# Reordering the output products, the rotation and the low parts around a layer's attention

## The chip, the cores and the metric

One core of a Trainium2 chip runs the whole program. The metric is the device time of one execution in microseconds; the number compared is the median of several executions.

## The reference, cut to what matters

The reference is a two-layer block followed by a second block (dilated attention, an RWKV mixer and a mixture of experts). The change touches only the two layers. One of them computes, for 256 tokens of width 1024 in float32:

```python
for l in range(2):
    h = rmsnorm(x, g_mix[l])
    cq, ckv, kr, aq, ak, av, qi, ki, wi, rq, rk, rv, rg = split(h @ w_in[l])
    q  = rmsnorm(cq, g_q[l]) @ w_uq[l]           # 8 heads of 64 + 32 rotated channels
    kv = rmsnorm(ckv, g_kv[l]) @ w_ukv[l]
    o_a = mla_attention(q, kv, rope(kr))         # 8 heads, 512 columns, causal softmax
    o_b = dsa_attention(aq, ak, av, top-64 keys by qi, ki, wi)   # 4 heads, 256 columns ("sparse")
    o_c = silu(rg) * head_groupnorm(retention(rq, rk, rv))       # 4 heads, 256 columns
    x = x + concat(o_a, o_b, o_c) @ w_out[l]     # 1024 x 1024
    x = x + square(relu(rmsnorm(x, g_mlp[l]) @ w_ff1[l])) @ w_ff2[l]
```

## The kernel before

**Precision.** A float32 product is made of three TensorE products of a "high" part (rounded to a short float) and a "low" part (value minus high part): high by high, high by low, low by high (lines 1101 to 1103). ScalarE makes the high part of a weight piece (line 2040), then GpSimd (or, for some pieces, VectorE) makes the low part (line 908); the same is done for activations when they leave PSUM: ScalarE writes the high part (lines 2014 and 2098), VectorE the low part (lines 2028 and 2624).

**Weights.** They come in pieces of 128 x 2048 words through three raw buffers and three split buffers, in the order of `layer_pieces()`: ..., `uq` 0 to 2, `ukv`, then `w_out` as `("out", c, i)` with c the half of the output columns and i the half of the rows, in the order (0,1), (1,1), (0,0), (1,0), then `ff1` and `ff2`. On ScalarE `split_after(name)` makes the high parts up to the piece three after `name`. So `split_after("ukv", 0, 0)` makes that of `out(0,0)`, `split_after("out", 0, 1)` that of `out(1,0)`, `split_after("out", 1, 1)` that of `ff1(0,0)`, `split_after("out", 0, 0)` that of `ff1(0,1)`. GpSimd takes its low parts in the order of the pieces, four instructions each; the low part of `ff1(0,1)` is VectorE's.

**The attention's stages.** Scores are made in ten groups: groups 0 to 3 are the sparse heads; 4 and 5 the eight MLA heads of the first 128 tokens; 6 to 9 pairs of MLA heads of the second 128 tokens. A group g passes through: score products on TensorE (line 1186, unit `("S", g)`), mask and row maximum on VectorE (`mask_scores`, line 2606), exponentials in place on ScalarE (`exponentials`, line 2090), scaling by the reciprocal sum on VectorE (`norm_probs`, lines 2615 and 2618), transposes on TensorE (`turn_probs`, line 1202, unit `("PT", g)`), copy out on ScalarE (`empty_turned`, line 2060), products with the values on TensorE (`attend_values`, line 1216 or 1220, unit `("O", g)`), high part on ScalarE (`high_values`, line 2098) and low part on VectorE (`low_values`, line 2624). The results lie in `hTq` as eight chunks of 128 rows: chunks 0 to 3 MLA, 4 and 5 sparse, 6 and 7 retention. The retention chunks come through `turn_retained` (line 1228, unit `("mixT", 3)`) and lines 2014 and 2028.

**Output products.** `project_out(c, i, t, ks)` multiplies chunks 4i + k, k in ks, of token half t by piece `out(c, i)` and adds into one PSUM bank per (c, t), `("wout", 2c + t)`: six products of 512 columns for two k, twelve for four. `add_out(u)` (line 2717) adds the finished bank to x on VectorE. x is then transposed (`tr3`, line 1074; first half of its columns needs `wout` 0 and 1, second half 2 and 3), split into high and low parts by ScalarE and VectorE, and the feed-forward products begin (lines 1396 and 1398).

**Order.** Each engine runs one queue, in the order written out by hand; engines meet through semaphores that count. `layer_plan()` lists the PSUM units in the order in which TensorE finishes them, with the bank and the engine (A ScalarE, V VectorE) that empties it; `units.begin(key)` waits until the bank's previous unit is emptied. `("O", 0)`, `("mlaT", 0)`, `("O", 2)` and `("wout", 0)` follow each other in bank 4. Before the MLA groups, the q channels are rotated on VectorE (`rotate`, lines 2449 to 2456, which waits for `uq`), q and kv are transposed on TensorE (`mlaT`, lines 1333 and 1341) and copied out (lines 2696 and 2179).

Of the kernel before, what the change touches and what calls it, by code (L numbers as in the profile page):

```python
# [324 lines left out]
def layer_plan():  # L325
# [4 lines left out]
    values = {g: ("O", g, 4 if g < N_DSA else (6, 7)[g % 2], "V") for g in VALUE_UNITS}  # L330
# [11 lines left out]
    plan += [("mlaT", j, 4 + j, "V") for j in range(4)] + [values[2]] + [("mlaT", 4 + j, j, "A") for j in range(4)]  # L342
    wout, turned_x = [("wout", u, (4, 5, 1, 3)[u], "V") for u in range(2 * T)], interleave("tr3", 4, (2, 0, 6, 7), "V")
    plan += [scores[4], scores[5], ("mixT", 3, 7, "V"), turned[4], scores[6], turned[5], values[4], scores[7], turned[6], values[5], scores[8], turned[7], values[6], scores[9]]
    plan += [wout[0], turned[8], values[7], wout[2], turned[9], values[8], values[9], wout[1]] + turned_x[:2] + [wout[3]] + turned_x[2:]
    for b in range(FFB):
        plan += [("ff1", 2 * b + j, ((0, 1), (2, 3))[j], "V") for j in range(2)]
    plan += interleave("ff2", 2 * T, (4, 5, 6, 7), "V")
# [234 lines left out]
def program(nc, io, out):  # L583
    tables = shape_tables()
    with ExitStack() as ctx:
# [510 lines left out]
        def _(pe):  # L1096
# [41 lines left out]
            with pe.Fori(0, DEPTH) as l:  # L1138
# [92 lines left out]
                def project_out(c, i, t, ks, last_of_piece=False):  # L1231

                    w = arrived(("out", c, i))
                    key = ("wout", T * c + t)
                    bank = units.begin(key) if i == 1 and ks[0] == 0 else units.bank(key)
                    for k in ks:
                        ins = product(bank, [hTq[:, which, 4 * i + k, t * P:(t + 1) * P] for which in range(2)],
                                      [x_[:, k, :] for x_ in w], i == 1 and k == 0, i == 0 and k == 3)
                    if i == 0 and ks[-1] == 3:
                        units.finish(key, ins)  # L1240
                    if last_of_piece:
                        read(("out", c, i), ins)
# [100 lines left out]
                def attend_mla(g):  # L1343
                    t, first_head = GROUPS[g][1], GROUPS[g][2][0]
                    units.wait_emptied(*(("mlaT", 4 * m + 2 * tt + first_head // 4) for m in range(2) for tt in range(t + 1)))
                    attend_scores(g)

                attend_mla(4)
                attend_mla(5)
                ret_ready.wait(pe, 1, l)  # L1350
                turn_retained()
                units.wait_emptied(("O", 0), ("mixT", 3))
                project_out(0, 1, 0, range(4))
                units.wait_emptied(("O", 2))
                project_out(0, 1, 1, range(4), True)
                turn_probs(4)
                attend_mla(6)
                turn_probs(5)
# [11 lines left out]
                attend_mla(9)  # L1370
                project_out(0, 0, 0, (2, 3))
                turn_probs(8)
                attend_values(7)
                project_out(1, 0, 0, range(4))
                turn_probs(9)
                attend_values(8)
                units.wait_emptied(("O", 6), ("O", 7))
# [3 lines left out]
                project_out(0, 0, 1, (2,))  # L1381
                units.wait_emptied(("O", 9))
                project_out(0, 0, 1, (3,))
                project_out(1, 0, 1, (0, 1))
                units.wait_emptied(("wout", 0), ("wout", 1))
                transposes(pe, units, "tr3", x, (0, 1))
                project_out(1, 0, 1, (2, 3))

                def ff1_part(b, j, f, ks):

# [655 lines left out]
        def _(act):  # L2046
# [3 lines left out]
            with act.Fori(0, DEPTH) as l:  # L2050
# [11 lines left out]
                def split_after(*name):  # L2062
                    split_high(LW.index[name] + SPLITS)
# [120 lines left out]
                exponentials(4)  # L2184
                exponentials(5)
                empty_turned(4)
                split_after("ukv", 0, 0)
                empty_turned(5)
                exponentials(6)
                high_values(4)  # L2190
                split_after("out", 0, 1)
                empty_turned(6)
                exponentials(7)
                high_values(5)
                empty_turned(7)
                exponentials(8)
                high_values(6)
                split_after("out", 1, 1)
                empty_turned(8)
                exponentials(9)  # L2200
                high_values(7)
                empty_turned(9)
                high_values(8)
# [331 lines left out]
        def _(dve):  # L2535
# [7 lines left out]
            for l in range(DEPTH):  # L2543
# [144 lines left out]
                mask_scores(3)  # L2688
                norm_probs(2)
                norm_probs(3)  # L2690
                low_values(0)
                units.wait_emptied(*(("uq", j) for j in range(2 * T)))
                rotate(dve, *halves(q[:, :, :, NOPE:QK]), *angles(ROPE), q_tmp).then_inc(q_roped.sem, 1)
                for j in range(4):
                    bank = units.wait_full(("mlaT", j))
                    units.emptied_by(("mlaT", j), dve.tensor_copy(
                        qTm[0:QK, 4 * (j % 2):4 * (j % 2) + 4, j // 2 * P:(j // 2 + 1) * P],
                        bank[0:QK, :].rearrange("p (c s) -> p c s", c=4)), "V")
# [20 lines left out]
                norm_probs(4)  # L2719
                norm_probs(5)  # L2720
                mask_scores(6)
                low_values(4)
                norm_probs(6)
                mask_scores(7)
                low_values(5)
                norm_probs(7)
                mask_scores(8)
                low_values(6)
                norm_probs(8)
                mask_scores(9)  # L2730
                add_out(0)
                low_values(7)
                norm_probs(9)
                add_out(2)
                low_values(8)
                low_values(9)
                add_out(1)
                low_transposed(dve, units, "tr3", 2, gain(G_MLP), hTp, hT_hi, l, (0, 1), 1)
                add_out(3)
                split_low(LW, dve, LW.index["ff1", 0, 1], l)  # L2740
# [596 lines left out]
```

## Time and profile before

| | us |
|---|---|
| median of 3 runs | 1397.04 (1396.71 to 1401.29) |
| the profiled execution | 1395.43 |
| its span, first to last instruction | 1393.4 |
| busy: PE / DVE / ACT / POOL | 1347.1 / 622.7 / 541.0 / 449.3 |
| granted TensorE clock, mean | 0.998 |

PE is TensorE, PEld its weight loads, DVE VectorE, ACT ScalarE, POOL GpSimd. Busy times are unions of the instructions' spans on that engine. The profiled execution is 2.0 us longer than its span, and 1.6 us below the median. The first layer's attention and output products lie between 96 and 161 us of the span, the second layer's 328.3 us later.

### The profile page before, as it was taken

What the parts mean: (1) busy time and instruction counts of PE and PEld (TensorE: products, weight loads), DVE (VectorE), ACT (ScalarE), POOL (GpSimd) and SP (SyncE); (2) the same over time, 40 slices, a digit from 0 to 9 for tenths busy, and PEclk for the clock granted to TensorE, in tenths of its full rate; (3) what the DMA queues carried; (4) which work ended last, traced back from release to release, by engine and by line L of the source; (5) the groups of instructions that cost most, each with busy time, mean ns of one, the idle gap of its engine ahead of it and who ended that gap; (6) DMA issues with size and microseconds to landing.
All of it is one profiled execution on the core that took longest, in us unless ns stands there. A gap on an engine that the chain in (4) does not pass through costs nothing.

```text
span 1393.4 us, 19892 instructions
## 1 busy us (share of the span) xinstructions
PE 1347.1 (97%) x7754; PEld 931.0 (67%) x7754; DVE 622.7 (45%) x1060; ACT 541.0 (39%) x790; POOL 449.3 (32%) x295
## 2 busy tenths in 40 slices
PE   8998999999999999999999999999999999999998
PEld 7786788887887788888887877755434444344343
DVE  5685554544687455353344887523202112122021
ACT  6667644435576654343555562212111111111011
POOL 2384454444374544543867913000000000000000
PEclk9999999999999999999999999999999999999999
DMA  7441454553533355455786351479999999999997
GB/s 289 137 168 67 152 181 181 185 202 127 207 116 110 116 204 190 181 182 181 237 278 225 103 208 52 137 290 411 422 428 428 427 428 428 428 427 427 428 423 292
DMA packets 50250, 351.99 MB, mean 253 GB/s; under 512 B 7747, under 2 KB 9679, under 8 KB 25583
## 3 DMA queue, kind: packets, MB, share of 16 engines
q1 hardware_dynamic: 49438, 349.52, 64.9%
q8 instruction: 63, 1.03, 0.3%
q10 hardware_dynamic: 720, 1.20, 0.2%
q14 instruction: 29, 0.24, 0.0%
HBM read 347.78 MB, written 1.07 MB: 250 GB/s over the span
## 4 chain that ended last, share of the span: by engine, by line
PE 72%; DMA 11%; DVE 7%; ACT 3%; issue 3%; DVEq 2%; POOL 1%; SPq 0%; ACTq 0%; POOLq 0%
PE psum L1925 12%; PE psum L1101 9%; PE psum L1103 9%; PE psum L1102 9%; PE psum L1396 9%; DMA ring<-in_w_expert_up 8%; PE psum L1946 5%; PE psum L1398 4%; PE psum L1091 4%; PE psum L1853 2%; POOL weights_split L908 1%; PE psum L1863 1%; DMA arena<-in_w_expert_down 1%; DVE arena L2577 1%; ACT weights_split L2040 1%
## 5 line engine op out<-in xcount | busy, mean ns | idle before, releaser
L908 POOL TENSOR_TENSOR weights_split<-weights_raw,weights_split 128x512 fp32r<-128x512 f32 (+2 forms) x253 | 401.6, 1621 | 338.2 <-ACT weights_split L2040 338.2
L2040 ACT ACTIVATE weights_split<-weights_raw 128x2048 fp32r<-128x2048 f32 (+4 forms) x154 | 243.5, 1586 | 243.5 <-PE psum L1103 145.3
L1925 PE MATMUL psum<-ring,arena 128*64 128x512 f32 x944 | 226.5, 598 | 12.1 <-DMA ring<-in_w_expert_up 11.2
L1396 PE MATMUL psum<-h_split,weights_split 128*128 128x512 f32 x512 | 182.1, 399 | 3.1 <-DVE h_split L2028 2.7
L1925 PEld LDWEIGHTS psum<-ring,arena 128*64 128x64 f32 x944 | 73.4, 138 | 136.4 <-issue 135.8
L1101 PE MATMUL psum<-weights_split,h_split 128*128 128x512 f32 (+3 forms) x400 | 151.9, 380 | 4.3 <-POOL weights_split L908 2.4
L1101 PE MATMUL psum<-weights_split,hidden_split 128*128 128x512 f32 (+1 forms) x384 | 151.1, 393 | 4.3 <-DVE hidden_split L2028 4.3
L908 DVE TENSOR_TENSOR weights_split<-weights_raw,weights_split 128x2048 fp32r<-128x2048 f32 (+3 forms) x53 | 119.3, 2257 | 70.1 <-ACT weights_split L2040 68.3
L1102 PE MATMUL psum<-weights_split,h_split 128*128 128x512 f32 (+3 forms) x400 | 149.5, 374 | 0.0
L1103 PE MATMUL psum<-weights_split,h_split 128*128 128x512 f32 (+3 forms) x400 | 149.2, 373 | 0.0
L1103 PE MATMUL psum<-weights_split,hidden_split 128*128 128x512 f32 (+1 forms) x384 | 147.3, 384 | 0.0
L1102 PE MATMUL psum<-weights_split,hidden_split 128*128 128x512 f32 (+1 forms) x384 | 147.1, 383 | 0.0
L1398 PE MATMUL psum<-h_split,weights_split 128*128 128x256 f32 x512 | 143.7, 281 | 0.0
L1946 PE MATMUL psum<-arena 128*64 128x512 f32 x512 | 113.4, 595 | 4.3 <-ACT arena L2433 3.7
L1396 PEld LDWEIGHTS psum<-h_split,weights_split 128*128 128x128 f32 x512 | 96.2, 188 | 28.5 <-issue 2.7
L3273 DVE TENSOR_TENSOR arena<-psum,arena 128x512 f32<-128x512 f32 x16 | 11.1, 691 | 219.4 <-PE psum L1925 219.4
L1398 PEld LDWEIGHTS psum<-h_split,weights_split 128*128 128x128 f32 x512 | 96.7, 189 | 0.5
L1101 PEld LDWEIGHTS psum<-weights_split,h_split 128*128 128x128 f32 x400 | 75.3, 188 | 22.6 <-issue 4.4
L1101 PEld LDWEIGHTS psum<-weights_split,hidden_split 128*128 128x128 f32 x384 | 72.1, 188 | 22.1 <-issue 7.3
L1103 PEld LDWEIGHTS psum<-weights_split,h_split 128*128 128x128 f32 x400 | 75.2, 188 | 13.9
L1102 PEld LDWEIGHTS psum<-weights_split,h_split 128*128 128x128 f32 x400 | 75.3, 188 | 12.9 <-issue 0.2
L1946 PEld LDWEIGHTS psum<-arena 128*64 128x64 f32 x512 | 35.8, 137 | 71.6 <-issue 63.5
(379 smaller groups left out, 1734.5 us busy)
## 6 DMA issues: line engine op xcount, KB each, us to landing
weights_raw<-in_layer_w SPq DMA_DIRECT2D x94, 1024.0 KB, 4.8
arena<-in_w_expert_down SPq DMA_DIRECT2D x28, 2048.0 KB, 14.7
ring<-in_w_expert_up SPq DMA_DIRECT2D x28, 2048.0 KB, 15.0
ring<-in_w_expert_gate SPq DMA_DIRECT2D x23, 2048.0 KB, 16.2
weights_raw<-in_second_w SPq DMA_DIRECT2D x44, 512.0 KB, 4.7
arena<-in_w_expert_gate SPq DMA_DIRECT2D x4, 2048.0 KB, 10.2
ring<-in_w_expert_up SPq DMA_DIRECT2D x8, 1024.0 KB, 13.1
arena<-in_w_expert_down SPq DMA_DIRECT2D x16, 512.0 KB, 12.3
```

Source lines behind the costliest of these rows:

```text
L908: ins = eng.tensor_tensor(W.part(j, 1, n)[:, cols], W.raw(j, n)[:, cols], W.part(j, 0, n).bitcast(F32)[:, cols], ALU.subtract)
L1091: ins = pe.matmul(bank[:, 0:n], lhs(i), w[:, i, :], start=(i == 0), stop=(i == k - 1))
L1101: pe.matmul(out, a[0], b[0], start=first, stop=False)
L1102: pe.matmul(out, a[0], b[1], start=False, stop=False)
L1103: return pe.matmul(out, a[1], b[0], start=False, stop=last)
L1396: pe.matmul(both.rearrange("p (w s) -> p w s", w=2), w[0][:, k, f * P:(f + 1) * P], hTp[:, :, k, :], start=(k == 0), stop=False)
L1398: ins = pe.matmul(both[:, 0:SEQ], w[1][:, k, f * P:(f + 1) * P], hTp[:, 0, k, :], start=False, stop=(k == KD - 1))
L1853: ins = pe.matmul(bank[:, kk * 2 * P:(kk + 1) * 2 * P], rows[:, t, k * P:(k + 1) * P], take_pair[:, t, :, :].rearrange("p j n -> p (j n)") ...
L1863: ins = pe.matmul(final.bank(("acc", 2 * t + c)), takeT[:, t * P:(t + 1) * P], y_parts[:, part, c * 512:(c + 1) * 512], start=False, stop= ...
L1925: ins = pe.matmul(bank[half(j), :], xe[h][:, k, half(j)], w[j][:, k, :], start=(k == 0), stop=(k == KD - 1))
L1946: ins = pe.matmul(banks[c][half(j), :], hidT[:, f, half(j)], w[j][:, f, c * 512:(c + 1) * 512], start=(f == 0), stop=(f == D_EXP // P - 1))
L2040: act.activation(W.part(j, 0, w), W.raw(j, w), ACT.Copy).then_inc(W.hi, 1)
```

## The change

On TensorE, `project_out` for the sparse chunks of both token halves (k 0 and 1 of `out(0,1)`) goes ahead of and behind `turn_retained`, and that for the retention chunks (k 2 and 3) behind both; later, `out(1,0)` of the first token half is cut in two, the first half goes ahead of `attend_values(7)`, the second behind the last products of `out(0,0)`, and all of the second token half's goes behind the first transposes of x. `layer_plan()` lists `("wout", 2)` behind `("wout", 1)` to match. On VectorE the rotation of q goes ahead of `low_values(0)`, `norm_probs(g)` ahead of `low_values(g - 2)` for g = 6 to 9, and `add_out(2)` behind `add_out(1)`. On ScalarE the high parts of `out(0,0)` and `out(1,0)` go behind `exponentials(6)` and `exponentials(7)` with what follows these, and `exponentials(9)` ahead of `empty_turned(8)`. No instruction is added or taken away but for waits; the number of matrix products is the same.

```diff
@@ -342,7 +342,7 @@
     plan += [("mlaT", j, 4 + j, "V") for j in range(4)] + [values[2]] + [("mlaT", 4 + j, j, "A") for j in range(4)]
     wout, turned_x = [("wout", u, (4, 5, 1, 3)[u], "V") for u in range(2 * T)], interleave("tr3", 4, (2, 0, 6, 7), "V")
     plan += [scores[4], scores[5], ("mixT", 3, 7, "V"), turned[4], scores[6], turned[5], values[4], scores[7], turned[6], values[5], scores[8], turned[7], values[6], scores[9]]
-    plan += [wout[0], turned[8], values[7], wout[2], turned[9], values[8], values[9], wout[1]] + turned_x[:2] + [wout[3]] + turned_x[2:]
+    plan += [wout[0], turned[8], values[7], turned[9], values[8], values[9], wout[1], wout[2]] + turned_x[:2] + [wout[3]] + turned_x[2:]
     for b in range(FFB):
         plan += [("ff1", 2 * b + j, ((0, 1), (2, 3))[j], "V") for j in range(2)]
     plan += interleave("ff2", 2 * T, (4, 5, 6, 7), "V")
@@ -1347,12 +1347,15 @@
 
                 attend_mla(4)
                 attend_mla(5)
+                units.wait_emptied(("O", 0))
+                project_out(0, 1, 0, (0, 1))
                 ret_ready.wait(pe, 1, l)
                 turn_retained()
-                units.wait_emptied(("O", 0), ("mixT", 3))
-                project_out(0, 1, 0, range(4))
                 units.wait_emptied(("O", 2))
-                project_out(0, 1, 1, range(4), True)
+                project_out(0, 1, 1, (0, 1))
+                units.wait_emptied(("mixT", 3))
+                project_out(0, 1, 0, (2, 3))
+                project_out(0, 1, 1, (2, 3), True)
                 turn_probs(4)
                 attend_mla(6)
                 turn_probs(5)
@@ -1370,8 +1373,8 @@
                 attend_mla(9)
                 project_out(0, 0, 0, (2, 3))
                 turn_probs(8)
+                project_out(1, 0, 0, (0, 1))
                 attend_values(7)
-                project_out(1, 0, 0, range(4))
                 turn_probs(9)
                 attend_values(8)
                 units.wait_emptied(("O", 6), ("O", 7))
@@ -1381,10 +1384,10 @@
                 project_out(0, 0, 1, (2,))
                 units.wait_emptied(("O", 9))
                 project_out(0, 0, 1, (3,))
-                project_out(1, 0, 1, (0, 1))
+                project_out(1, 0, 0, (2, 3))
                 units.wait_emptied(("wout", 0), ("wout", 1))
                 transposes(pe, units, "tr3", x, (0, 1))
-                project_out(1, 0, 1, (2, 3))
+                project_out(1, 0, 1, range(4))
 
                 def ff1_part(b, j, f, ks):
 
@@ -2184,20 +2187,20 @@
                 exponentials(4)
                 exponentials(5)
                 empty_turned(4)
-                split_after("ukv", 0, 0)
                 empty_turned(5)
                 exponentials(6)
                 high_values(4)
-                split_after("out", 0, 1)
+                split_after("ukv", 0, 0)
                 empty_turned(6)
                 exponentials(7)
                 high_values(5)
+                split_after("out", 0, 1)
                 empty_turned(7)
                 exponentials(8)
                 high_values(6)
                 split_after("out", 1, 1)
+                exponentials(9)
                 empty_turned(8)
-                exponentials(9)
                 high_values(7)
                 empty_turned(9)
                 high_values(8)
@@ -2688,9 +2691,9 @@
                 mask_scores(3)
                 norm_probs(2)
                 norm_probs(3)
-                low_values(0)
                 units.wait_emptied(*(("uq", j) for j in range(2 * T)))
                 rotate(dve, *halves(q[:, :, :, NOPE:QK]), *angles(ROPE), q_tmp).then_inc(q_roped.sem, 1)
+                low_values(0)
                 for j in range(4):
                     bank = units.wait_full(("mlaT", j))
                     units.emptied_by(("mlaT", j), dve.tensor_copy(
@@ -2719,22 +2722,22 @@
                 norm_probs(4)
                 norm_probs(5)
                 mask_scores(6)
+                norm_probs(6)
                 low_values(4)
-                norm_probs(6)
                 mask_scores(7)
+                norm_probs(7)
                 low_values(5)
-                norm_probs(7)
                 mask_scores(8)
+                norm_probs(8)
                 low_values(6)
-                norm_probs(8)
                 mask_scores(9)
                 add_out(0)
+                norm_probs(9)
                 low_values(7)
-                norm_probs(9)
-                add_out(2)
                 low_values(8)
                 low_values(9)
                 add_out(1)
+                add_out(2)
                 low_transposed(dve, units, "tr3", 2, gain(G_MLP), hTp, hT_hi, l, (0, 1), 1)
                 add_out(3)
                 split_low(LW, dve, LW.index["ff1", 0, 1], l)
```

## Rows read from the trace of the kernel before

**Rows 1.** The page's groups of instructions: busy us, mean ns | idle before.
```profile
L1102 PE MATMUL psum<-weights_split,hidden_split 128*128 128x512 f32 (+1 forms) x384 | 147.1, 383 | 0.0
```
**Rows 2.** PE's waits, whole execution: total us, times, longest.
```profile
PE psum L1101 <- DVE hidden_split L2028: 4.3, 2, 2.2
...
PE psum L1333 <- DVE arena L2456: 2.6, 2, 1.3
...
PE psum L1202 <- DVE arena L2618: 2.4, 2, 1.2
```
**Rows 3.** Windows of both attention stages and one feed-forward: length, then busy times.
```profile
107.70:161.00 53.30, 47.07 (x286) 36.93 (x285) 29.25 (x79) 34.32 (x71) 25.29 (x18) 1.00 0.26 85
435.90:489.30 53.40, 47.20 (x287) 36.98 (x286) 29.23 (x79) 34.35 (x72) 25.32 (x18) 1.00 0.26 86
161.00:336.00 175.00, 175.00 (x880) 147.78 (x879) 82.67 (x68) 73.16 (x55) 81.85 (x60) 1.00 0.53 190
```
**Rows 4.** Timeline of PE, first layer: start, duration, instruction, [idle before <- releaser].
```profile
110.07 1.95 PE L1333 MATMUL psum<-shared_c,arena 128*96 128x128 f32 x16 [1.33 <-DVE arena L2456]
...
116.54 0.60 PE L1228 MATMUL psum<-shared_c,arena 128*128 128x128 f32 x4
119.31 0.49 PE L1101 MATMUL psum<-weights_split,hidden_split 128*128 128x512 f32 x1 [2.17 <-DVE hidden_split L2028]
...
124.88 0.60 PE L1202 MATMUL psum<-shared_c,arena 128*128 128x128 f32 x4
...
130.16 1.03 PE L1186 MATMUL psum<-arena 96*128 96x256 f32 x4
132.39 0.65 PE L1202 MATMUL psum<-shared_c,arena 128*128 128x128 f32 x4 [1.20 <-DVE arena L2618]
...
142.17 0.60 PE L1202 MATMUL psum<-shared_c,arena 128*128 128x128 f32 x4
...
152.65 1.03 PE L1074 MATMUL psum<-shared_c,xs 128*128 128x128 f32 x8
...
156.01 0.49 PE L1396 MATMUL psum<-h_split,weights_split 128*128 128x512 f32 x1 [0.94 <-DVE h_split L2028]
...
158.74 0.50 PE L1396 MATMUL psum<-h_split,weights_split 128*128 128x512 f32 x1 [0.19 <-DVE weights_split L908]
...
160.80 0.50 PE L1396 MATMUL psum<-h_split,weights_split 128*128 128x512 f32 x1 [0.41 <-DVE h_split L2028]
```
**Rows 5.** Timeline of DVE, same stage.
```profile
107.18 0.42 DVE L2624 TENSOR_TENSOR hidden_split<-psum,hidden_split 128x256 fp32r<-128x256 f32 x1 [0.81 <-ACT hidden_split L2098]
...
109.52 0.42 DVE L2456 TENSOR_TENSOR arena<-arena 128x256 f32<-128x256 f32 x1
...
121.48 1.62 DVE L2618 TENSOR_TENSOR arena<-arena,stat 128x512 f32<-128x512 f32 x1
...
123.30 0.69 DVE L2618 TENSOR_TENSOR arena<-arena,stat 128x512 f32<-128x512 f32 x1
...
156.40 2.28 DVE L908 TENSOR_TENSOR weights_split<-weights_raw,weights_split 128x2048 fp32r<-128x2048 f32 x1
159.09 1.66 DVE L2028 SCALAR_TENSOR_TENSOR h_split<-psum,gains,h_split 128x256 fp32r<-128x256 f32 x4 [0.41 <-ACT h_split L2014]
```
**Rows 6.** One line, DVE's scaling, 100 to 150 us: min/median/max ns.
```profile
L2618 DVE TENSOR_TENSOR arena<-arena,stat x8: 691/692/1721, 104.4 to 145.4; 128x512 f32<-128x512 f32 x8
```
**Rows 7.** Timeline of ACT, same stage.
```profile
117.37 0.83 ACT L2014 ACTIVATE hidden_split<-psum,gains 128x256 fp32r<-128x256 f32 x2
...
126.02 1.90 ACT L2040 ACTIVATE weights_split<-weights_raw 128x2048 fp32r<-128x2048 f32 x1
```
**Rows 8.** Timeline of POOL, same stage.
```profile
117.56 4.99 POOL L908 TENSOR_TENSOR weights_split<-weights_raw,weights_split 128x512 fp32r<-128x512 f32 x4 [16.62 <-ACT weights_split L2040]
128.00 10.94 POOL L908 TENSOR_TENSOR weights_split<-weights_raw,weights_split 128x512 fp32r<-128x512 f32 x8 [5.45 <-ACT weights_split L2040]
```
**Rows 9.** One line, POOL's low parts, 157 to 164 us: min/median/max ns.
```profile
L908 POOL TENSOR_TENSOR weights_split<-weights_raw,weights_split x4: 1272/1284/2722, 157.1 to 162.3; 128x512 fp32r<-128x512 f32 x4
```

## The prediction

> **What bounds the kernel now.** The page first: TensorE is busy 1347.1 of 1393.4 us, so only its holes can be won by a reordering. The list of what TensorE waited for shows where they are: three kinds, each met twice, once per layer, make 9.3 us: the retention chunks' low parts 4.3, the rotation of q 2.6, the scaling of the probabilities 2.4 [rows 2]. The windows show the two attention stages alike (47.07 of 53.30 us and 47.20 of 53.40 busy), so I follow the first layer and double; and a feed-forward stage behind with TensorE busy 175.00 of 175.00 [rows 3], whose length a shift of its start does not change. The timelines place the holes: 1.33 us before 110.07, 2.17 before 119.31, 1.20 before 132.39, then 0.94, 0.19 and 0.41 where the feed-forward begins [rows 4]; 6.24 in all. A closed hole gives about 0.15 more than its bracket: 24 products start 5.57/24 = 0.23 apart between 119.31 and 124.88 [rows 4], but one has a mean duration of 0.383 [rows 1], so in a packed run the next starts 0.15 before the modelled end. After small operations I count a run of n products as 0.23n + 0.1.
>
> **The change part by part**, in the first layer's times; new times leave out the shift of the step before.
>
> *Rotation ahead of `low_values(0)`.* The rotation ends at 109.94 and TensorE starts at 110.07. Ahead of it stand the low part's wait of 0.81 (for ScalarE's high part) and its instruction, issued at 107.18, the rotation's first 0.34 later [rows 5]. VectorE would be free at 107.18 - 0.81 = 106.37; the rotation starts then and not at 107.52, some 1.2 earlier. But the first transposes of q go to bank 4, which unit `("O", 0)` must leave, and `low_values(0)` empties it, now behind the rotation: 0.34 given back. TensorE could start at 108.74 (110.07 - 1.33), and starts near 109.2. **-0.89.** Bounds: 0 if something else held it, -1.33 if all of it goes. `low_values(0)` itself is needed by nothing earlier.
>
> *Sparse chunks first.* Before: transposes at 116.54, hole 2.17, 24 products from 119.31, `turn_probs(4)` at 124.88. After: six products 116.54 to 118.04, transposes to 118.56 (modelled end 118.64), six more products to 120.06. ScalarE's high part of the retention chunks, started at 117.37 [rows 7] when ScalarE came free, must now wait for the transposes: 118.68, 1.31 later. So the chunks are ready at 119.31 + 1.31 = 120.62, a wait of 0.56 is left, and twelve products end at 120.62 + 2.86 = 123.48, against 124.88. **-1.40** (the 1.6 of hole that close, less one more opening of a run and rounding).
>
> *What is late next.* The exponentials of groups 4 and 5 stand behind that high part on ScalarE, so they too are 1.31 later, and VectorE's scalings go from 121.48 to 122.79 and from 123.30 to 124.61 [rows 5]. The first took 1.62, against a median of 0.692 [rows 6]: GpSimd's four low parts ran to 117.56 + 4.99 = 122.55 [rows 8]. At 122.79 GpSimd is just done, I take 0.69, and `turn_probs(4)` starts at 123.58: +0.10. Behind it come four transposes and four score products, 1.31, so TensorE is at `turn_probs(5)` at 124.89; the scaling of group 5 ends at 125.30: **+0.50**, together **+0.60**. Bounds: 0 if ScalarE is not late, +1.6 if the first scaling meets GpSimd again (1.03 more).
>
> *High part of `out(0,0)` behind the exponentials, scaling ahead of the low part.* The scaling of group 6 now stands behind ScalarE's 1.90 of high part [rows 7] ahead of the exponentials and behind `low_values(4)`. Without both, exponentials start behind the copy of PT(5), near 126.5, and the scaling runs 127.8 to 128.5. TensorE is at `turn_probs(6)` at 125.4 + (132.39 - 1.35 - 126.19) = 130.2 (126.19 is 124.88 + 1.31). The whole hole goes: 1.20 + 0.15, **-1.35**, with 1.7 to spare, so a meeting with GpSimd does no harm here.
>
> *What that makes late.* The high part of `out(0,0)` starts not at 126.02 but behind `high_values(4)`, near 128.1, so GpSimd's eight instructions for `out(0,0)` and `out(1,0)` start at 130.0 instead of 128.00 and end, at 10.94 [rows 8], at 140.9; `out(1,0)`'s high part, done near 134.8, is before GpSimd wants it. `turn_probs(8)` comes at 142.17 - 2.15 = 140.02 (2.15 is 1.40 - 0.60 + 1.35). `out(0,0)` is needed 3.8 before that, 136.2, and ready at 135.5. `out(1,0)` is needed right behind it, since its first half goes ahead of `attend_values(7)`: at 140.54, against 140.9, or 140.0 if no instruction meets VectorE's. **+0.2**, between 0 and 0.4. `norm_probs(9)` now runs beside the low part of `ff1(0,0)` and may end up to 0.7 late for `turn_probs(9)` or not at all: I take what the small hole near 146 gives back, **0**.
>
> *Second token half's products last.* Before, x's first transposes at 152.65 were followed by six products, and their low parts were ready 3.36 later, at 156.01 [rows 4]. Now 12 products follow (0.5 to 0.8 of transposes and 2.86), 3.6 in all: TensorE never waits. 0.94 + 0.15, **-1.09**; bounds -0.5 and -1.1. `add_out(2)` sits in VectorE's idle time ahead of those low parts.
>
> *Start of the feed-forward.* Count from its first product (156.01 before). The last bank of the output is now full only there; `add_out(3)` 0.6, then VectorE's low part of `ff1(0,1)`, 2.28 [rows 5]: ready 3.15 after the start, against 2.73 (158.74) before. Then the low parts of x's second half, which took 160.80 - 159.09 = 1.71 to reach TensorE [rows 4, 5]: 4.85 after the start, against 4.79. **+0.05**; between -0.3 and +0.4.
>
> Sum for a layer: -0.89 - 1.40 + 0.60 - 1.35 + 0.20 + 0 - 1.09 + 0.05 = -3.88; for both -7.8. The profiled execution took 1395.43 (span 1393.4), so 1387.7 for one like it; the median of the runs is 1397.04, and there I forecast 1389.3. I take the second, since the comparison is of medians. The parts behind the layers follow TensorE through semaphores and keep their length.
>
> A row and a rule: the eight scalings have a median of 692 ns and a maximum of 1721 [rows 6], and the one at 121.48 ended 0.55 after GpSimd's last instruction. The Trainium skill, SBUF — State Buffer, section Who interferes with whom, says that VectorE with two inputs in SBUF and GpSimd share one pair of ports as an exclusive lock: the second to start stands still until the first is done. By that rule, the trace agrees here, a scaling waits for at most one GpSimd instruction of 1.28; this speaks for the bound of +1.6 above if GpSimd runs 0.25 later than I think, and is priced in the first rival.
>
> **Rivals.** (1) *The scaling meets GpSimd.* The reordering puts ScalarE's late exponentials and GpSimd's late low parts on the path. For it: 122.79 is only 0.24 behind GpSimd's end; `out(1,0)` is already at its limit; two of the known scalings were long. Against: most were not. Price per layer: +1.0 at group 4, +0.2 for `out(1,0)`, +0.7 at `turn_probs(9)`: -3.88 + 1.9 = -2.0, 1393.0 in all. Chance 0.17. (2) *Other side: GpSimd's low parts of the output's pieces become the bound.* They start 2.0 later, and TensorE comes earlier. GpSimd's instruction can last 2.72 instead of 1.28 beside VectorE's [rows 9]; if all eight did, they would end at 130.0 + 21.8 = 151.8, 11.3 after 140.54, giving -3.9 + 11.1 = +7.2 per layer, 1411. It decides from a mean of 1.32 per instruction and turns the sign from about 1.8 (eight at 1.8 end at 144.4). Against: the eight took 1.37 on average [rows 8], and VectorE has fewer than ten shared operations there. Chance 0.03. (3) *It closes more than I count*: ScalarE is not late, or a hole of mine does not open. All of 6.24 plus 0.15 for each goes, less 0.25 of openings: -6.9, 1383.2 at the utmost; half way, -5.3 a layer, 1386.4. Chance 0.12. (4) *It does not do what it says*: each hole is filled by the next releaser, or the second block, where weights stream, takes the shift back; the windows tell against it for the layers only [rows 3]. 1397.0. Chance 0.06. The forecast has 0.62, with its own range of 1387.5 to 1391.5.
>
> **How the numbers follow.** A measurement of this kernel tells 0.3%, 4.2 us, from no change, so faster is below 1392.8. Forecast and rival 3 give 0.74; rival 1 is at the border and gives 0.09; 0.83 faster, 0.14 same, 0.03 slower. The range of 8 in 10 takes rival 3's half way point at one end and rival 1 at the other: 1386.2 to 1393.2.
>
> **What the changed profile would show.** TensorE's wait for the rotation shrinks from 1.33 to about 0.4 and names `low_values`' line 2624. The 2.17 wait becomes about 0.5 at the retention chunks' products. Waits for line 2618 stand at `turn_probs(4)` (0.1) and `turn_probs(5)` (0.5), not at 6. The wait of 0.94 for line 2028 is gone; one for line 908 on VectorE of some 0.8 stands at `ff1(0,1)`. GpSimd starts `out(0,0)` 2 us later relative to `turn_retained`. TensorE's idle time between the transposes of q and the steady feed-forward falls from 6.2 to about 2.5 a layer. I am wrong if a wait for GpSimd's line 908 of more than 1 us appears, or if the two stages shorten by less than 2 us each.

## The result and the profile after

The median is 1388.76 us (16 executions, 1387.03 to 1396.30) against 1397.47 us for the kernel before in the same comparison (16 executions, 1394.50 to 1402.71): ratio 0.9943, 95% interval 0.9928 to 0.9958, faster by 8.0 us. The profiled execution took 1389.37 us, its span 1387.3.

Measured from the same two events in each layer (from the eight transposes ahead of the q transposes to VectorE's first feed-forward reduction, line 2754 before and 2757 after), this "stage" was 57.64 and 57.60 us long before. The windows of the stage, before and then after (length, then busy PE, PEld, DVE, ACT, POOL, granted clock, DMA share, GB/s):

```profile
107.71:165.35 57.64, 51.41 (x310) 40.71 (x309) 29.24 (x80) 38.27 (x79) 27.86 (x20) 1.00 0.29 95
436.01:493.61 57.60, 51.40 (x310) 40.71 (x309) 29.12 (x79) 38.27 (x78) 27.87 (x20) 1.00 0.29 95
```

```profile
107.86:162.46 54.60, 51.41 (x310) 40.47 (x309) 29.60 (x77) 38.45 (x78) 27.12 (x20) 1.00 0.30 99
432.33:485.96 53.63, 51.35 (x310) 40.56 (x309) 28.61 (x77) 38.46 (x78) 27.11 (x20) 1.00 0.30 101
```

TensorE is busy for as long as before, so what went is its idle time. The first layer gave 3.04 us, the second 3.97. They were alike before [rows 3] and are not now. Timeline of TensorE after, first layer: the entries with a wait, and three without one, which had a wait before or stand where a product was moved [rows 4]:

```profile
109.26 1.95 PE L1333 MATMUL psum<-shared_c,arena 128*96 128x128 f32 x16 [0.36 <-DVE hidden_split L2627]
...
119.63 0.51 PE L1101 MATMUL psum<-weights_split,hidden_split 128*128 128x512 f32 x1 [0.52 <-DVE hidden_split L2031]
...
122.70 0.65 PE L1202 MATMUL psum<-shared_c,arena 128*128 128x128 f32 x4
...
124.52 0.65 PE L1202 MATMUL psum<-shared_c,arena 128*128 128x128 f32 x4 [0.30 <-DVE arena L2621]
...
129.41 0.60 PE L1202 MATMUL psum<-shared_c,arena 128*128 128x128 f32 x4
...
140.16 0.50 PE L1101 MATMUL psum<-weights_split,hidden_split 128*128 128x512 f32 x1 [0.38 <-POOL weights_split L908]
...
143.27 0.65 PE L1202 MATMUL psum<-shared_c,arena 128*128 128x128 f32 x4 [0.87 <-DVE arena L2621]
...
149.63 1.03 PE L1074 MATMUL psum<-shared_c,xs 128*128 128x128 f32 x8
...
156.42 0.50 PE L1399 MATMUL psum<-h_split,weights_split 128*128 128x512 f32 x1 [0.71 <-DVE weights_split L908]
```

The waits of 1.33, 2.17, 1.20 and 0.94 have become 0.36, 0.52, none and none; group 5's transposes wait 0.30, `out(1,0)` 0.38, group 9's transposes 0.87, `ff1(0,1)` 0.71. Second layer, three of the same places:

```profile
448.94 0.65 PE L1202 MATMUL psum<-shared_c,arena 128*128 128x128 f32 x4 [0.30 <-DVE arena L2621]
...
464.58 0.50 PE L1101 MATMUL psum<-weights_split,hidden_split 128*128 128x512 f32 x1 [0.39 <-POOL weights_split L908]
...
479.92 0.50 PE L1399 MATMUL psum<-h_split,weights_split 128*128 128x512 f32 x1 [0.70 <-DVE weights_split L908]
```

All as in the first layer, but no wait for group 9. VectorE shows why; reciprocal and scaling of group 8, then the scaling of group 9, in each layer:

```profile
136.56 0.17 DVE L2618 RECIPROCAL stat<-stat 128x2 f32<-128x2 f32 x1 [1.29 <-ACTq L2095]
137.15 1.82 DVE L2621 TENSOR_TENSOR arena<-arena,stat 128x512 f32<-128x512 f32 x1 [0.42 <-issue]
...
141.32 1.82 DVE L2621 TENSOR_TENSOR arena<-arena,stat 128x512 f32<-128x512 f32 x1
...
460.98 0.17 DVE L2618 RECIPROCAL stat<-stat 128x2 f32<-128x2 f32 x1 [1.29 <-ACTq L2095]
461.22 0.91 DVE L2621 TENSOR_TENSOR arena<-arena,stat 128x512 f32<-128x512 f32 x1
...
464.66 1.67 DVE L2621 TENSOR_TENSOR arena<-arena,stat 128x512 f32<-128x512 f32 x1
```

In the first layer the scaling of group 8 starts 0.59 behind its reciprocal, in the second 0.24. GpSimd's instructions beside it, first layer and second:

```profile
137.11 1.30 POOL L908 TENSOR_TENSOR weights_split<-weights_raw,weights_split 128x512 fp32r<-128x512 f32 x1
...
461.53 1.76 POOL L908 TENSOR_TENSOR weights_split<-weights_raw,weights_split 128x512 fp32r<-128x512 f32 x1
```

In both layers GpSimd's next instruction starts 0.55 behind the reciprocal. In the second layer the scaling was issued ahead of that: it stands still for 0.2 (0.91 instead of 0.69), and then GpSimd is the one that is held (1.76 instead of 1.30). In the first it comes 0.04 behind GpSimd's start and stands still for 1.1. So group 9's scaling follows 1.1 earlier in the second layer (3.68 behind group 8's reciprocal, not 4.76). GpSimd, first layer, is busy without a break through all this: its `out(0,0)`, `out(1,0)` and `ff1(0,0)` now come as one run, where [rows 8] had eight instructions from 128.00 and then a pause.

```profile
116.75 5.02 POOL L908 TENSOR_TENSOR weights_split<-weights_raw,weights_split 128x512 fp32r<-128x512 f32 x4 [15.66 <-ACT weights_split L2043]
129.21 16.31 POOL L908 TENSOR_TENSOR weights_split<-weights_raw,weights_split 128x512 fp32r<-128x512 f32 x12 [7.45 <-ACT weights_split L2043]
```

Eleven more kernels were run, and the kernel after once more. Unless said otherwise there is one profiled execution of each, and the number compared is the stage's length in the two layers. It repeats: the kernel after, run again, gave 54.52 and 53.61.

### The profile page after: what moved, and what is told of

It reads as the page before. It is cut to its first block, busy times and chain, and to the rows that moved or that the text cites. A ratio compares the mean times of both kernels' runs of the same rounds, so it can differ in the third digit from the quotient of the medians.

```text
span 1387.3 us, 19894 instructions
## 1 busy us (share of the span) xinstructions
PE 1345.5 (97%) x7754; PEld 929.8 (67%) x7754; DVE 623.9 (45%) x1060; ACT 541.2 (39%) x790; POOL 449.0 (32%) x295
## 4 chain that ended last, share of the span: by engine, by line
PE 72%; DMA 10%; DVE 7%; ACT 3%; DVEq 2%; issue 2%; POOL 2%; ACTq 1%; SPq 0%; POOLq 0%
PE psum L1928 13%; PE psum L1101 9%; PE psum L1399 9%; PE psum L1103 8%; PE psum L1102 8%; DMA ring<-in_w_expert_up 8%; PE psum L1949 5%; PE psum L1401 4%; PE psum L1091 4%; PE psum L1856 2%; POOL weights_split L908 2%; PE psum L1866 2%; DVE arena L2580 1%; DMA arena<-arena 1%; ACT weights_split L2043 1%
```

## Experiments: each part alone, on the kernel before

**The rotation alone.**

```diff
-low_values(0)
 rotate(dve, *halves(q[:, :, :, NOPE:QK]), *angles(ROPE), q_tmp).then_inc(q_roped.sem, 1)
+low_values(0)
```

> The kernel before with the rotation alone moved ahead of low_values(0). Measured is the stage length in the trace: from the eight transposes ahead of the q transposes to VectorE's first feed-forward reduction; before 57.64 and 57.60 us in the two layers, after 54.60 and 53.63. Theory (each part closes its own hole, and its gain is kept): 0.95 less per stage, 56.7 in both, wait before the q transposes 0.36 instead of 1.33, all other waits as before. Rival (the holes are one chain of ScalarE and VectorE, and what one gives is taken by the next): the wait before the retention chunks' products or before the scaling of group 6 grows by 0.9 and the stage stays at 57.6.

Measured 56.59 in the first layer (-1.05), with a wait of 0.32 and all others as before. The second layer took 58.21 with the same waits: there the granted clock of TensorE fell behind the 2.16 wait (see the section on the clock).

**The sparse chunks first, alone** (the first change of TensorE's order, no other).

> The kernel before with TensorE's order at the retention chunks alone changed (sparse chunks' products ahead of and behind the transposes). Theory: wait before the retention chunks' products 0.5 instead of 2.17, but ScalarE comes 1.3 late to group 4's exponentials, so 0.5 comes back at the transposes of group 5 and the wait before group 6's stays near 1 us: stage 56.5 (1.1 less). Rival (the hole is closed and all of it is kept): 1.7 to 2.2 less, 55.4 to 55.9. Rival (absorbed by group 6's wait): 57.6.

Measured 56.43 and 56.44 (-1.2), with waits of 0.51 at the retention chunks, 0.30 at group 5 and 0.82 at group 6, as the theory had it. From start to start, TensorE came to group 4's transposes 1.38 earlier, lost 0.51 again up to group 5's, and won 0.31 up to group 6's, whose wait fell from 1.20 to 0.82.

**ScalarE's and VectorE's order alone.**

> The kernel before with ScalarE's and VectorE's order of groups 6 to 9 alone changed (high parts behind exponentials, scaling ahead of low parts). Theory: the wait of 1.20 before group 6's transposes goes, no wait for GpSimd appears since TensorE reaches the first product of out(1,0) at 141.9 and it is ready by 141.8: stage 56.3 (1.3 less), at most 57.0 if a scaling meets GpSimd's instruction. Rival (GpSimd's later low parts are the new bound): wait for line 908 of 1 us or more, 57.3 or longer.

Measured 56.02 in the first layer (-1.6), with no wait for group 6 and none of TensorE for GpSimd. The second layer took 57.67, again with a fall of the clock behind the 2.16 wait. The rival, GpSimd as the new bound, is refuted.

**The late products alone**, with `layer_plan()` and `add_out(2)` moved to match (not shown).

```diff
-attend_values(7)
-project_out(1, 0, 0, range(4))
+project_out(1, 0, 0, (0, 1))
+attend_values(7)
...
-project_out(1, 0, 1, (0, 1))
+project_out(1, 0, 0, (2, 3))
 transposes(pe, units, "tr3", x, (0, 1))
-project_out(1, 0, 1, (2, 3))
+project_out(1, 0, 1, range(4))
```

> The kernel before with TensorE's late products alone moved (out(1,0) of the first token half cut in two, all of the second half's behind the first transposes of x; bank order and add_out(2) to match). Theory (the parts depend on each other): the scaling of group 9 still stands behind low_values(7), which now waits for products that come 1.5 us later, so a wait of 1.5 to 2.3 opens at group 9's transposes; the wait of 0.94 at the feed-forward goes: stage 57.8 to 58.8, that is not shorter. Rival (parts are independent and add): 1.0 less, 56.6.

Measured 62.14 and 60.38: slower, as expected, but by more than the 57.8 to 58.8 of the theory. TensorE, second layer:

```profile
480.06 0.65 PE L1202 MATMUL psum<-shared_c,arena 128*128 128x128 f32 x4 [2.73 <-DVE arena L2618]
480.64 0.66 PE L1220 MATMUL psum<-arena 128*64 128x128 f32 x8
481.23 0.53 PE L1101 MATMUL psum<-weights_split,hidden_split 128*128 128x512 f32 x1
481.57 0.62 PE L1102 MATMUL psum<-weights_split,hidden_split 128*128 128x512 f32 x1
481.99 0.63 PE L1103 MATMUL psum<-weights_split,hidden_split 128*128 128x512 f32 x1
```

A wait at group 9's transposes was expected, of 1.5 to 2.3; it is 2.73. That the products behind it start 0.42 apart instead of 0.23 was not expected: the clock fell there, in both layers, and in the first layer behind the 2.16 wait as well. Less 1.6 for each of these falls (a price taken from the two runs above) the stages would be near 58.8 and 58.9. To part the two effects:

**The late products with group 9's scaling ahead of `low_values(7)`.** Against the run just shown:

```diff
-low_values(7)
 norm_probs(9)
+low_values(7)
```

> The kernel with the late products alone, and group 9's scaling put ahead of low_values(7) as in the kernel after. Theory (the late products were slower alone only because the scaling of group 9 stood behind low_values(7), and because a wait of 2.73 is followed by the lower clock): the wait at group 9's transposes falls from 2.73 to about 1.4 (group 9's scaling still meets GpSimd), no clock below 1 behind it, stage 57.4 to 58.0 against 62.14 and 60.38. Rival (the late products are slow in themselves): 59 or more.

Measured 57.72 and 57.71, with a wait of 1.51 at group 9's transposes and the clock at 1.00 throughout both stages. So VectorE's order, with the falls of the clock behind its long wait, made the late products slow. With that order mended they alone are worth nothing (+0.1): what they save at the feed-forward, where the wait of 0.94 for x's low parts is gone and one of 0.71 for `ff1(0,1)` has come, they pay at group 9.

## Experiments: what is left in the kernel after

**The transposes first again.**

```diff
-project_out(0, 1, 0, (0, 1))
 ret_ready.wait(pe, 1, l)
 turn_retained()
+project_out(0, 1, 0, (0, 1))
```

> The kernel after, but the retention chunks' transposes go first and both token halves' sparse products behind them. Theory (the leftover waits of 0.52 and 0.30 come from ScalarE being 1.3 late because the transposes stand behind six products): both waits go, though group 4's scaling meets GpSimd again (1.6 us) and a wait of 0.2 may open at group 4: 0.6 less than after, 54.0 and 53.0. Rival (what is left is the fixed path through ScalarE and VectorE, not the place of the transposes): the wait stays at 0.5, stage 54.6 and 53.6.

Measured 53.08 and 53.03. The waits of 0.52 and 0.30 are gone, so they came from ScalarE being late. In their place stands:

```profile
122.63 0.65 PE L1202 MATMUL psum<-shared_c,arena 128*128 128x128 f32 x4 [0.70 <-DVE arena L2621]
```

Group 4's scaling meets GpSimd again, as at 121.48 in [rows 5] (here it took 1.68), and this costs 0.70 where I wrote 0.2. The first layer gained 1.5, since its wait of 0.87 also went. Group 8's scaling and GpSimd's instruction beside it show why:

```profile
136.56 0.69 DVE L2621 TENSOR_TENSOR arena<-arena,stat 128x512 f32<-128x512 f32 x1 [0.42 <-issue]
...
136.60 1.82 POOL L908 TENSOR_TENSOR weights_split<-weights_raw,weights_split 128x512 fp32r<-128x512 f32 x1
```

The scaling is again 0.59 behind its reciprocal, but now 0.04 ahead of GpSimd instead of 0.04 behind it. It takes 0.69, and GpSimd's instruction takes 1.82 instead of some 1.29. The order of the two starts decided, by hundredths of a us.

**The high part of `ff1(0,0)` behind `empty_turned(9)`**, so that GpSimd has nothing to do while group 9 is scaled.

> The kernel after, but ScalarE's high part of ff1(0,0) stands behind empty_turned(9), so GpSimd has nothing to do while group 9 is scaled. Theory (GpSimd's instruction makes the scaling 1.8 us long and holds it): group 9's scaling takes 0.69 in both layers, the wait of 0.87 at group 9's transposes in the first layer goes, stage 53.7 and 53.6, so the layers agree again. Rival (the scaling is long for another reason, such as ScalarE's or DMA traffic): it stays at 1.7 to 1.8 and 54.6.

Measured 53.92 and 53.91, the layers alike. Group 9's scaling:

```profile
140.95 0.69 DVE L2621 TENSOR_TENSOR arena<-arena,stat 128x512 f32<-128x512 f32 x1
```

1.82 became 0.69 at the same place, so GpSimd was what had held it. A wait of 0.28 for a low part (line 2627) appeared, which is why the second layer lost 0.3.

**GpSimd's steps halved** (`LOW_STEP = 256`). The scalings from 100 to 150 us (min/median/max ns), first in the kernel after, then here, and TensorE's wait for `out(1,0)`:

> The kernel after with GpSimd's low parts in the layers cut into steps of 256 columns instead of 512. Theory (a scaling waits for the rest of one GpSimd instruction): no scaling above 1.4 us (0.69 and one GpSimd instruction of about 0.7) where the longest was 1.82; GpSimd's piece gets some 0.5 us longer from the extra instructions, so the wait for out(1,0) grows to about 1.0: stage 54.0 to 55.2. Rival (shared bandwidth, not a wait for an instruction): the scalings keep up to 1.8.

```profile
L2621 DVE TENSOR_TENSOR arena<-arena,stat x8: 691/694/1820, 104.6 to 141.3; 128x512 f32<-128x512 f32 x8
```

```profile
L2621 DVE TENSOR_TENSOR arena<-arena,stat x8: 691/694/1037, 103.4 to 139.1; 128x512 f32<-128x512 f32 x8
```

```profile
140.61 0.50 PE L1101 MATMUL psum<-weights_split,hidden_split 128*128 128x512 f32 x1 [2.00 <-POOL weights_split L908]
```

The longest scaling fell from 1.82 to 1.04 (1.11 in the second layer): it waits for the rest of one GpSimd instruction, as under an exclusive lock; the rival, a shared bandwidth, had the scalings stay at up to 1.8. But 256 columns took GpSimd 0.73 (median) where 512 took 1.29, so the pieces came later, TensorE waited 2.00 for `out(1,0)`, and the stage grew to 55.21 and 55.17.

**More of `ff1(0,0)` ahead of `ff1(0,1)`** (not shown: its bank is reported as full only behind the last k).

```diff
 transposes(pe, units, "tr3", x, (2, 3))
+ff1_part(0, 0, 1, range(4))
 ff1_part(0, 1, 0, range(4))
...
-ff1_part(0, j, 1, range(KD))
+ff1_part(0, j, 1, range(4 if j == 0 else 0, KD))
```

> The kernel after, with the first four k of the second half of ff1(0,0) (1.4 us of products) ahead of ff1(0,1)'s. Theory (the wait of 0.71 is VectorE's low part of ff1(0,1), late by that much while its products could be replaced): the wait goes and none opens, 0.7 less in both layers, 53.9 and 52.9. Rival (VectorE's next low parts, of x's second half, are as late): the wait moves to the next products and the stage is within 0.2 of after.

Measured 53.42 and 52.50 (-1.18, -1.13), with no wait at the feed-forward. That is more than the 0.71 of the bracket. In the first layer the time from the start of x's second transposes to the first product behind them went from 1.74 to 0.79 us (-0.95), and the products up to the reduction gave 0.20 more, since they are now one packed run.

**The kernel after, again.**

> The kernel after, unchanged, to compare the others with on one chip. Theory: 8 to 9 us below before in the median, stage near 53.6 in both layers where group 9's scaling meets GpSimd late, 54.6 where it meets it for the whole instruction; the split between these may differ from the first profile (54.60, 53.63), because 0.1 us decides it. Rival (the two layers differ by their code, not by chance): again 54.6 in the first and 53.6 in the second.

Median 1388.07 (6 executions), ratio to before 0.9934 (0.9913 to 0.9955); stages 54.52 and 53.61. The theory left the difference between the layers to chance; it repeats, also in the kernel with more of `ff1(0,0)` first. The 0.59 from reciprocal to scaling of group 8 (136.36 to 136.95 here) stands in the first layer of seven traces and in the second of none: both of this kernel, the order alone, and the four kernels of this section. VectorE's program is written out once per layer, so the two layers are different places in it. The place alone is not the cause, though: the version with all edits (next section) has VectorE's instructions in the same order, and there the scaling follows 0.24 behind in both layers. What the 0.42 of "issue" is was not tested.

## Experiments: the clock behind a hole, and the best version

Ten stages have the wait of 2.16 to 2.17 (before, rotation alone, order alone, late products, late products with group 9). Three of them had a low clock right behind it: the second layer of the rotation alone and of the order alone, and the first of the late products. Both stages with the wait of 2.73 had one behind that. Windows that start where TensorE comes back from the wait, or up to 0.3 behind, second layer: the kernel before, the rotation alone, the late products behind 2.73:

```profile
447.60:451.00 3.40, 3.40 (x15) 2.83 (x16) 1.42 (x2) 3.22 (x16) 3.24 (x3) 1.00 0.00 0
```

```profile
445.40:448.40 3.00, 3.00 (x8) 2.31 (x8) 1.27 (x2) 2.83 (x15) 2.95 (x3) 0.50 0.00 0
```

```profile
480.00:483.00 3.00, 2.94 (x17) 2.27 (x18) 0.29 (x1) 0.87 (x2) 0.00 (x0) 0.76 0.88 276
```

Before, TensorE runs 15 products in 3.4 us at full clock; in the second window 8 in 3.0, at a granted clock of 0.50, the lower of its two levels, 1.2 GHz. Each fall cost about 1.6 us (58.21 - 56.59; 57.67 - 56.02). The eighteen stages with waits of 2.00 at most had none.

The length of the wait does not settle it, and the falls are not confined to these stages. Windows of the rotation alone ahead of and in one fall, and of one fall each in the second block of the kernel before and the kernel after:

```profile
954.10:957.10 3.00, 2.10 (x15) 1.79 (x14) 2.76 (x13) 1.08 (x3) 0.00 (x0) 1.00 1.00 418
957.50:960.50 3.00, 3.00 (x16) 3.00 (x16) 1.35 (x8) 1.24 (x2) 0.00 (x0) 0.50 1.01 431
...
1043.80:1046.80 3.00, 3.00 (x10) 0.87 (x8) 0.00 (x0) 0.00 (x0) 0.00 (x0) 0.50 1.03 437
...
1253.60:1256.60 3.00, 3.00 (x8) 0.95 (x10) 0.00 (x0) 0.00 (x0) 0.00 (x0) 0.50 1.00 426
```

TensorE's only wait over 0.4 us between 943 and 957 was one of 0.90. The other two falls stand behind waits of 2.68 and 2.39 for weights.

**The hole filled.** The kernel before, with four products whose results are overwritten (eight instructions in the trace):

```diff
 turn_retained()
+bridge(pe, units, ("wout", 0), 4)
 units.wait_emptied(("O", 0), ("mixT", 3))
```

> The kernel before with four products of 256 columns, whose results are overwritten, put in TensorE's wait of 2.17 before the retention chunks' products. In three of eight stages with that wait the granted clock was about 0.6 for some 3 us behind it (kernels with the rotation, the engines' order and the late products alone), and never behind waits of 2.00 or less. Theory (an idle TensorE of 2.2 us is sometimes followed by the lower clock, so the hole costs more than its length): the wait shrinks to about 0.4, stage 57.6 as before, no stage of the trace longer, and the median is 0.5 to 2 us below before. Rival (the clock falls for reasons of its own): median as before within 0.5 and the spread of the runs as wide.

```profile
116.88 1.89 PE L1065 MATMUL psum<-shared_c 128*128 128x256 f32 x8
119.20 0.49 PE L1101 MATMUL psum<-weights_split,hidden_split 128*128 128x512 f32 x1 [0.43 <-DVE hidden_split L2029]
```

Median 1394.90 (12 executions, 1393.60 to 1396.35) against 1397.10 (17, 1394.40 to 1403.11): ratio 0.9982 (0.9969 to 0.9995), so 2.2 us by the medians, a little more than the 0.5 to 2 of the theory. The stage kept its length (57.49, 57.45) and nothing in it came more than 0.15 earlier; what went is the upper part of the spread. Ten of the 17 executions before are above 1396.35, the slowest of the twelve with the filler. The granted clock over a whole execution agrees: 0.9964 in the mean of the 17, 0.9982 in that of the twelve, and 0.0018 of 1395 us is 2.5 us. So the hole cost more in the median than its own length, and a kernel that closes it can win something that the profiles of before and after, both without a fall in these stages, can't show. Single falls can't be assigned: the profile with the filler has two in the second block besides the one at the program's end that every profile has, and the kernel after still had an execution of 1396.30.

**All together**: transposes first, group 6's scores ahead of group 4's transposes, the high part of `out(0,0)` right behind `exponentials(6)`, that of `ff1(0,0)` behind `empty_turned(9)`, more of `ff1(0,0)` first.

> The kernel after with all that the runs so far point to: retention transposes first, group 6's scores ahead of group 4's transposes, high part of out(0,0) right behind exponentials(6), that of ff1(0,0) behind empty_turned(9), more of ff1(0,0) ahead of ff1(0,1). Theory (the leftover waits have separate causes and each edit takes its own): stage 51.2 to 52.0 in both layers (after 54.60 and 53.63), no TensorE wait above 0.5 but the one before the q transposes, profiled execution near 1384, median 5 us below that of after. Rival (the waits replace each other, as in the kernel with the late products alone): stage 53 or more, median within 2 us of after.

```profile
107.98:159.12 51.14, 50.31 (x310) 40.91 (x309) 29.10 (x77) 37.11 (x76) 26.75 (x20) 1.00 0.30 104
428.85:480.01 51.16, 50.25 (x310) 40.87 (x309) 29.13 (x77) 37.08 (x76) 26.76 (x20) 1.00 0.31 104
```

Median 1381.79 (6 executions), ratio to before 0.9897 (0.9871 to 0.9922), 6.3 us below the kernel after beside it. The stages took 51.14 and 51.16, just under the 51.2 to 52.0 of the theory, and TensorE's waits are 0.32, 0.20 and 0.28 in the first, 0.34, 0.25 and 0.29 in the second. Five of the six executions are faster than every one of the kernel after beside it.

## Why the prediction was right

1389.3 was forecast, 1388.76 measured; -7.8 forecast, -8.0 by the ratio. Step by step, from start to start in the traces (the last step from 152.65 to the reduction at 165.35 before, 149.63 to 162.46 after, less 1.36 for the six more products that now lie in it; the two ahead of it are the brackets):

| step | forecast | layer 1 | layer 2 |
|---|---|---|---|
| rotation ahead | -0.89 | -0.96 | -0.98 |
| sparse chunks first, with group 4 | -1.30 | -1.37 | -1.37 |
| group 5's transposes late | +0.50 | +0.51 | +0.51 |
| group 6's hole | -1.35 | -1.31 | -1.31 |
| `out(1,0)` from GpSimd | +0.20 | +0.38 | +0.39 |
| group 9's transposes | 0 | +0.87 | 0 |
| products behind x's transposes, feed-forward | -1.04 | -1.2 | -1.2 |
| stage | -3.88 | -3.04 | -3.97 |

The mechanism held at every line but one. In the sum itself the waits add up as they should: TensorE's brackets in a stage went from 6.24 to 3.14 and 2.23, where about 2.5 was forecast. The step that was mis-sized is "`norm_probs(9)` ... may end up to 0.7 late ... I take 0": the first layer paid 0.87, a price that rival 1 had named. What made it go the one way or the other is whether VectorE's scaling of group 8 or GpSimd's next instruction comes first. The 0.35 us of VectorE's issue put it 0.04 behind, and the trace before, where this scaling follows 0.24 and 0.23 behind its reciprocal, could not show that. Smaller: `out(1,0)` cost 0.38 of the 0 to 0.4 allowed, not 0.20. One sign was put wrongly: GpSimd starts `out(0,0)` 2.0 later in the stage, as forecast, once the rotation's shift of 0.96 is taken out (21.35 into the stage, where it was 20.29 before), but only 0.6 later relative to `turn_retained`, which itself moved behind six products.

The stages gave 7.0, not 7.8, and the rest was made up elsewhere. The two profiled executions differ by 6.1 (1395.43 to 1389.37): the time between the two stages was 0.8 shorter, that ahead of the first 0.15 longer and that behind the second 1.6 longer, though no code was changed there. The kernel after, profiled again, took 1387.15, so this is from run to run. The ratio gives 8.0 here and 9.2 in the second comparison. The filled hole shows where 1 to 2 us above the stages can come from: the falls of the clock behind the 2.17 wait, which I had not counted. For the change itself this share is an estimate, since no run took the falls out of it. So the number came out nearer than its sum deserved, and that is luck.

Against rival 2, GpSimd ended its run of twelve at 145.5 and cost 0.38. Rival 3 (more closes than counted) is refuted for this kernel and true of the code: 2.5 to 3.5 us more per layer were there, by other edits. Rival 4 is refuted by the length of the stages.

I had treated the late products as worth 1.09. Their hole closed, but alone they are worth nothing (+0.1) with group 9's scaling ahead, and cost 2.8 and 4.5 without it, falls of the clock included. What they are worth in the whole stays open. By the table they give nothing in the first layer (+0.38 + 0.87 - 1.2) and 0.8 in the second (+0.39 - 1.2). But the other three parts alone sum to -3.9, so by that sum they give 0.1 in the second layer and cost 0.8 in the first. The kernel after without them was not run.

## What to carry to other kernels

When an order is changed on several engines at once, write down for each moved instruction who is queued behind it on its engine: here the late products did not pay until VectorE's scaling was moved ahead, and the waits of 0.52 and 0.30 left over were ScalarE's queue behind a transpose. Let the work that another engine waits for go first, and fill the wait with products behind it, not ahead of it. A meeting of VectorE and GpSimd costs up to one of GpSimd's instructions; here it paid to give GpSimd later the work that nobody waits for yet (1.82 to 0.69 for the scaling, 0.7 off the first layer, though 0.3 lost in the second), and shorter steps did not (0.6 and 1.5 lost).

## What the runs showed of the hardware

- A VectorE scaling of two SBUF inputs took 0.69 alone, up to 1.82 beside GpSimd's low parts of 1.29, and at most 1.11 beside those of 0.73. The Trainium skill, SBUF — State Buffer, Who interferes with whom, has this as an exclusive lock held for the whole instruction; the runs agree.
- It holds both ways: GpSimd's instruction took 1.76 and 1.82 where VectorE's scaling was first. At 0.04 us behind GpSimd's start the scaling took 1.82, at 0.04 ahead of it 0.69.
- GpSimd took 1.29 for 512 columns and 0.73 for 256. As an estimate from these two, about 0.17 of an instruction does not shrink with its columns.
- An idle TensorE of 2.2 us was followed by the lower clock for about 3 us in three of ten stages, at some 1.6 us each; windows of 3 to 4 us over these falls show 0.50, 0.59 and 0.62 in the mean. Behind one of 2.7 us there was a fall in both stages that had it (0.76 and 0.67 in the two windows of 3 us behind it in the second layer). The sixteen stages whose longest wait was 1.33 or less had no such fall, nor the two with 2.00; but elsewhere in the program one stood behind a wait of 0.90.
